# Sample attention of a two-layer decoder step: queries as stationary operand on four column quarters, one reversed scan, values of the own head

## The reference, cut to what matters

```python
z = jnp.einsum('bqkgd,bskd->bkgqs', qb, k) / math.sqrt(HEAD_DIM) + bias
mask = kpos[None, :] < qpos[:, None]
log_keep = jnp.where(mask, jax.nn.log_sigmoid(-z), 0.0)
suffix = lax.cumsum(log_keep, axis=4, reverse=True) - log_keep
attn = jnp.where(mask, jnp.exp(jax.nn.log_sigmoid(z) + suffix), 0.0)
o = jnp.einsum('bkgqs,bskd->bqkgd', attn, v)
```

## Time and profile before

| | us |
|---|---|
| median of 3 runs | 2024.17 (2018.96 to 2031.26) |
| the profiled execution | 2034.04 |
| its span | 2032.4 |
| in it: new tokens' part of the sample attention | 1581.6 to 1590.9 |
| pages' part of the sample attention | 1590.9 to 1787.6 |
| layer 1 out and the last norm | 1787.6 to 2032.4 |

### The profile page before, as it was taken

One profiled execution on the slowest core, in us unless ns is written; L12 is line 12 of the kernel. 1 busy time (PEld: TensorE's weight loads), 2 busy tenths in 40 slices (PEclk: granted clock), 3 DMA queues, 4 the chain that ended last, 5 costly groups with the idle time before them and its releaser, 6 DMA issues.

```text
span 2032.4 us, 35373 instructions
## 1 busy us (share of the span) xinstructions
PE 1847.5 (91%) x13466; PEld 1761.1 (87%) x13466; DVE 1126.7 (55%) x1844; ACT 785.6 (39%) x1132; POOL 272.0 (13%) x184
## 2 busy tenths in 40 slices
PE   4999999999997999947999999999997799899995
PEld 3899999999997999937989989999996676689993
DVE  4766666666666222296667577577576433442226
ACT  3244444444434222232555455465455222232222
POOL 4100000000000001133322322322321000001110
PEclk9999999999998999957999999999998677799995
DMA  5323232322322323342222222222224346412324
GB/s 194 95 88 89 84 92 83 90 85 84 92 67 59 92 83 92 106 151 83 76 61 63 85 63 69 79 73 63 84 63 133 106 146 181 148 53 85 91 84 154
DMA packets 278697, 191.50 MB, mean 94 GB/s; under 512 B 7899, under 2 KB 250715, under 8 KB 277979
## 3 DMA queue, kind: packets, MB, share of 16 engines
q1 hardware_dynamic: 277708, 188.03, 31.1%
q0 software_dynamic: 896, 2.23, 0.4%
HBM read 174.26 MB, written 15.97 MB: 94 GB/s over the span
## 4 chain that ended last, share of the span: by engine, by line
PE 74%; DVE 12%; issue 7%; ACT 6%; DMA 1%; POOL 0%; SPq 0%; ACTq 0%; DVEq 0%; POOLq 0%
PE PS L591 20%; PE PS L593 20%; PE PS L592 20%; PE Z L876 4%; PE PS L847 2%; PE PS L858 1%; PE Z L591 1%; PE Z L593 1%; PE Z L592 1%; DVE Y L1463 1%; ACT WS L937 1%; ACT L1122 1%; DVE WS L1241 1%; DMA prow<-in_state_h_dram 1%; DVE T L1503 1%
## 5 line engine op out<-in xcount | busy, mean ns | idle before, releaser
L591 PE MATMUL PS<-U,WS 128*128 128x272 f32 x3712 | 1089.3, 293 | 60.3 <-DVE U L1470 34.1
L593 PE MATMUL PS<-U,WS 128*128 128x272 f32 x3712 | 1085.2, 292 | 0.0
L592 PE MATMUL PS<-U,WS 128*128 128x272 f32 x3712 | 1081.7, 291 | 0.0
L591 PEld LDWEIGHTS PS<-U,WS 128*128 128x128 f32 x3712 | 712.0, 192 | 67.6 <-issue 35.5
L592 PEld LDWEIGHTS PS<-U,WS 128*128 128x128 f32 x3712 | 712.1, 192 | 0.8
L593 PEld LDWEIGHTS PS<-U,WS 128*128 128x128 f32 x3712 | 711.5, 192 | 0.0
L1241 DVE TENSOR_TENSOR WS<-raw,WS 128x1024 fp32r<-128x1024 f32 (+1 forms) x240 | 305.9, 1275 | 500.5 <-ACT WS L937 498.0
L937 ACT ACTIVATE WS<-raw 128x1024 fp32r<-128x1024 f32 (+1 forms) x240 | 246.7, 1028 | 601.8 <-PE PS L593 596.1
L506 POOL TENSOR_TENSOR raw<-raw,GN 128x1024 f32<-128x1024 f32 x80 | 159.6, 1996 | 436.2 <-DMA raw<-in_b_w_in_dram 340.6
L518 POOL TENSOR_TENSOR T<-T 128x544 f32<-128x544 f32 x60 | 88.4, 1473 | 379.4 <-ACT T L1033 376.9
L515 POOL COPY T<-T 128x544 f32<-128x544 f32 x4 | 3.2, 790 | 852.2 <-ACT T L1033 825.4
(11 more groups left out here) (212 smaller groups left out, 2025.9 us busy)
## 6 DMA issues: line engine op xcount, KB each, us to landing
raw<-in_a_w_in_dram SPq DMA_DIRECT2D x80, 512.0 KB, 3.8
raw<-in_b_w_in_dram SPq DMA_DIRECT2D x64, 512.0 KB, 4.1
raw<-in_a_w_out_dram SPq DMA_DIRECT2D x32, 512.0 KB, 3.8
raw<-in_b_w_out_dram SPq DMA_DIRECT2D x32, 512.0 KB, 3.8
KPG<-in_cache_k_dram SPq DMA_DIRECT2D x64, 256.0 KB, 2.9
VPG<-in_cache_v_dram SPq DMA_DIRECT2D x64, 256.0 KB, 2.9
T<-scratch_x SPq DMA_DIRECT2D x32, 272.0 KB, 2.9
scratch_x<-T SPq DMA_DIRECT2D x16, 272.0 KB, 2.1
```

Source lines behind the costliest of these rows:

```text
L591: pe.matmul(psum, w_hi, x_hi, start=first, stop=False)
L592: pe.matmul(psum, w_hi, x_lo, start=False, stop=False)
L593: return pe.matmul(psum, w_lo, x_hi, start=False, stop=last)
```

## The change

The sample attention is written anew; the projections, the prompt's attention and all else stay.

- One step is a half page position j (16 of them): four sequences. `key_turn` is the same four transposes per sequence. `scores` swaps the operands: the queries of one key/value head and sequence are stationary (32 columns, of which 16 are its own and 16 belong to the neighbour and are ignored), the 128 turned keys are the moving columns, and the four heads k write the partition quarters 32k to 32k+31 of one bank. Scores thus have queries on partitions and keys along the free axis.
- The later-key sum is one reversed `tensor_tensor_scan` over 512 elements (four sequences by 128 keys) on DVE, with a multiplier `RUN` that is 0 where a new sequence starts, and the carry of the page before added to the last key. The triangular products and the high and low split are gone.
- The weights must now be turned back (`weights_turn`, four transposes per half step) and copied by ACT (`weight_copy`) before `values`, which multiplies only the own head: 16 products per half step with 32 stationary columns and 128 moving ones, again on four partition quarters, accumulated over all pages in PSUM. `OA` and its additions are gone.
- Loads come in half steps of four pages, each with its own semaphore; keys of positions 1 and 2 first, then their values, then keys and values of the half steps in turn. The loop is unrolled and page numbers have fixed places.
- The new tokens are handled in 32-column tiles, with 32 small products and a handful of small DVE operations.

```diff
-                    for k in range(NKV):
-                        cols = slice(k * P + b * 16, k * P + b * 16 + 16)
-                        ins = pe.matmul(zs[:, slot, cols], KPT[:, b % 4, k * DH:(k + 1) * DH], QS[:, cols], start=True, stop=True)
+            def scores(c):
+                j, i = c // 4, c % 4
+                pe.wait_ge(kp_odd if c % 2 else kp_even, c // 2 + 1)
+                for k in range(NKV):
+                    ins = pe.matmul(SC[k * QW:(k + 1) * QW, j % 2, i * P:(i + 1) * P], query(k, j % 2 * 4 + i),
+                                    KPT[:, c % 4, k * DH:(k + 1) * DH], start=True, stop=True)
+                ins.then_inc(kp_used, 1)
-                for b in range(NB):
-                    v = VST[:, :] if isinstance(n, int) and n == 0 else VPG[:, slot, b, :]
-                    ins = pe.matmul(d_pair_bank(b // 2)[b % 2 * QR:(b % 2 + 1) * QR, :], T[:, 4, b * QR:(b + 1) * QR], v,
-                                    start=True, stop=True)
+            def weights_turn(j):
+                h = j % 2
+                pe.wait_ge(d_exp, j + 2)
+                pe.wait_ge(d_wt_out, j + 1)
+                for i in range(4):
+                    ins = pe.transpose(WT[:, h, i * P:(i + 1) * P], DW[h][:, i * P:(i + 1) * P], IDN[:])
+                ins.then_inc(d_wt, 1)
+            def weigh(h, i, b, v, first, last):
+                for k in range(NKV):
+                    ins = pe.matmul(OS[k * QW:(k + 1) * QW, h, i * P:(i + 1) * P], WPT[:, h, i * P + k * QW:i * P + (k + 1) * QW],
+                                    v[:, k * DH:(k + 1) * DH], start=first and i == 0, stop=last and i == 3, skip_group_check=True)
+                return ins
+            for j in range(NHALF):
+                half_scores(j)
...
+                if j >= 4:
+                    values(j - 4)
+                if j >= 3:
+                    weights_turn(j - 3)
+            def weight_copy(j):
+                act.wait_ge(d_wt, j + 2)
+                act.wait_ge(d_pv, j + 1)
+                nc.scalar.activation(WPT[:, j % 2, :], WT[:, j % 2], ACT.Copy).then_inc(d_wt_out, 1)
+            def run_sums(j):
+                V.tensor_tensor_scan(DI[j % 2][:, ::-1], RUN[:, ::-1], DL[j % 2][:, ::-1], 0.0, ALU.mult, ALU.add).then_inc(d_scan, 1)
+                dve.wait_ge(d_scan, j + 1)
+                V.tensor_tensor(DZ[j % 2], DZ[j % 2], DI[j % 2], ALU.subtract).then_inc(d_arg, 1)
+            def load_keys(n, h):
+                if n > 2:
+                    sp.wait_ge(kp_t, 8 * (n - 3) + 4 * h + 4)
+                load_pages(n, h, KPG, a["cache_k"], keys_in)
+            def load_values(n, h):
+                if n > 2:
+                    sp.wait_ge(d_pv, 2 * (n - 3) + h + 3)
+                load_pages(n, h, VPG, a["cache_v"], values_in)
```

More of the change, by code:

```diff
@@ L882, in _ @@
-            pe.wait_ge(strip_out, SE0)
-            for k in range(NKV):
-                ins = pe.matmul(zs[0:NS, 0, k * P:(k + 1) * P], KST[:, k, :], QS[:, k * P:(k + 1) * P], start=True, stop=True)
-            ins.then_inc(d_z, 1)
-            d_later_keys(0)
-            PAGES = 16 * NB
-            d_step(1, 1, PAGES, first=True)
-            with pe.Fori(1, NPAGE // 2) as i:
-                d_step(i * 2, 0, i * PAGES, i * PAGES)
-                d_step(i * 2 + 1, 1, i * PAGES + PAGES, i * PAGES)
@@ L902, in pair_e @@
+            for j in range(NHALF, NHALF + 4):
+                values(j - 4)
+                if j < NHALF + 3:
+                    weights_turn(j - 3)
+            for h in range(2):
+                pe.wait_ge(d_sums[h], 1)
+                for i in range(4):
+                    ins = pe.transpose(KT[:, h, i * P:(i + 1) * P], OE[h][:, i * P:(i + 1) * P], IDN[:])
+                ins.then_inc(d_turned, 1)
             def pair_e(i, first):
@@ L1196, in _, with key_copy @@
-            d_exps(0, NS)
-            with act.Fori(1, NPAGE + 1) as n:
-                steps.loop(n, 1, 2)
-                for b in range(0, NB, 2):
-                    act.wait_ge(kp_t, n * 8 + (b - 7))
-                    if b >= 4:
-                        act.wait_ge(kp_used, n * 8 + (b - 11))
-                    nc.scalar.activation(KPT[:, b % 4, :], d_bank(b), ACT.Copy).then_inc(kp_even, 1)
-                d_exps(n, P)
-            steps.leave(NPAGE)
+            def key_copy(c):
+                act.wait_ge(kp_t, c + 1)
+                if c >= 4:
+                    act.wait_ge(kp_used, c - 3)
+                nc.scalar.activation(KPT[:, c % 4, :], KT[:, c % 2], ACT.Copy).then_inc(kp_even, 1)
@@ L1208, in _ @@
+            act.wait_ge(d_pv, NHALF + 1)
+            nc.scalar.activation(OE[0], OS[:, 0], ACT.Copy).then_inc(d_sums[0], 1)
             act.wait_ge(d_out, 1)
@@ L1664, in _ @@
-            d_chain(0, 0, NS)
-            dve.wait_ge(d_cleared, 1)
-            with dve.Fori(0, NPAGE // 2) as i:
-                steps.loop(i, 0, 2)
-                for m in (1, 2):
-                    n = i * 2 + m
-                    for b in range(1, NB, 2):
-                        dve.wait_ge(kp_t, n * 8 + (b - 7))
-                        if b >= 4:
-                            dve.wait_ge(kp_used, n * 8 + (b - 11))
-                        V.tensor_copy(KPT[:, b % 4, :], d_bank(b)).then_inc(kp_odd, 1)
-                    d_chain(n, m % 2, P)
@@ new lines, in _ @@
+            new_tokens()
+            for j in range(NHALF + 2):
+                if j < NHALF:
+                    key_copy(4 * j + 1)
+                if j == 0:
+                    new_weights()
+                if 1 <= j <= NHALF:
+                    logits(j - 1)
+                if j >= 2:
+                    keep(j - 2)
+                if j < NHALF:
+                    key_copy(4 * j + 3)
+                if j >= 2:
+                    run_sums(j - 2)
+            dve.wait_ge(d_pv, NHALF + 2)
```

369 lines of the change are left out of this document (203 added, 166 removed).

## The result

The changed kernel takes 1959.32 us (median of 4 runs, 1956.68 to 1961.7), the kernel before took 2027.72 beside it: a ratio of 0.966 (95% interval 0.962 to 0.971), **68 us less**. The forecast was 42 us less, 1982; the time lies inside the range, and it is the time of the second rival (the clock stays at 2.4 GHz and SP's issuing binds, 1956).

What follows compares the result with a forecast made beforehand. PE was taken to bound the pages, with SP's issuing binding at the higher clock. Low-clock and high-clock sums gave gains of 16 and 68 us; the middle, 42 off 2024.17, gave 1982 us, range 1948 to 2014.

Steps and rivals of the forecast that it cites:

- the second rival: Pages' part: the clock stays at 2.4 GHz and SP's issuing of page loads binds; 68 us less, 1956 us; chance 0.2.
- PE bounds the pages, its work falls: Pages, per half step: PE's work falls from 8.2 to 5.1 us at 2.4 GHz, 9.4 us at 1.2 GHz.
- The quarters overlap fully: Scores and values on PE: four column quarters run side by side, 0.85 us each per half step, bounds 0.85 and 3.4.
- The price of the rival: Quarters not side by side: scores and values each 2.55 us more at 2.4 GHz, 5.1 at 1.2; about 2160 us; chance 0.07.
- Its threshold: Serial quarters turn the change into a loss once a half step costs over 12.3 us.
- Changes of shape: PE's switches between 128 and 32 columns, eight per half step: 0.15 us each at 2.4 GHz, 0.20 at 1.2.
- The hole: Between half steps PE waits for ACT's weight copy and key copy: 1.6 us each time.
- The start: New tokens' work ahead of the pages: 9.3 us as before, bounds 6 and 12, so pages begin at 1590.9.
- SP: SP's queue issues page loads at 1.105 us each, 8.8 us per half step, binding at the higher clock.
- The sum for the high clock: Pages' part at 2.4 GHz from step 1 on, paced by SP: the stage ends at 1720, a gain of 68 us.
- The clock: Pages' part: a mixed clock with a mean near 0.75, given 0.5, spread over 1962 to 2004 us.
- the middle of the two sums: Between stage ends of 1772 (all at 1.2 GHz) and 1720 (2.4 GHz): near 1746, 42 us less.

Runs made afterwards that it cites:

- one-quarter kernel: The changed kernel with a sequence's four score products on one column quarter and all value products of a half step on quarter 0: 2015.82 us, ratio 0.994.
- widened kernel before: The kernel before with 128 query columns instead of 16 streamed through each score product: 1995.46 us, ratio 0.987.

## Why the prediction was right, and where it was not

- **PE bounds the pages, its work falls.** Right. At 2.4 GHz the half step's work without the hole was forecast at 5.1 us and is 6.47 - 1.18 = 5.3 us. Key turns, scores, values and weight turns all lie within about 0.2 us of their terms; a sequence of turns and scores is 0.94 us where 0.44 + 0.21 + two changes of shape of 0.15 make 0.95.
- **The quarters overlap fully.** Right, 1.06 us for 32 records, where the two bounds were 0.85 and 3.4. The price of the rival was right too: 2.55 us more for each was forecast, and the one-quarter kernel shows 0.64 x 4 = 2.6 us for the scores. Its threshold was not: serial quarters leave the kernel just ahead of before, because the clock stays up (0.98), whereas I had them run at 1.2 GHz and lose 136 us. TensorE: Matmul & The Clock Gate in the Trainium skill (Part 3, The mechanism) says that weight loads go beside running products only where the row group differs. Here all products use all 128 rows, and a change of the column quarter alone takes a record with its load from 0.11 to 0.033 us, so the trace differs.
- **Changes of shape.** Idle PEld of 0.17 us ahead of scores and 0.20 ahead of turns, eight times in a half step; the term of 0.15 us each was right to within 0.05.
- **The hole.** The loop is as forecast, but 1.18 us rather than 1.6: ACT starts 0.04 us after PE's turn ends, and its second copy starts 0.49 us after the first (1650.53 to 1651.02) rather than 0.59 + 0.13. This is the term with the largest error on the path at 2.4 GHz, and the clock may have hung on it: with holes of 1.80 and of 2.44 us, and a longer second wait, the mean clock goes to 0.87 and 0.73.
- **The start.** 9.3 us was taken, with bounds of 6 and 12. The first turn stands 7.1 us earlier than before; the 64 small records of the new tokens (L904) take 1.03 us, and their DVE and ACT steps run beside the pages' first turns instead of ahead of them. From the end of the prompt's last product to the first turn it is 2.2 us (1582.58 to 1584.78), under the lower bound. That serial chain did not exist any more, which the bounds had missed.
- **SP.** Right: 1.12 us per page from 1620 to 1705 where 1.105 was taken, no pause, PE waiting for pages at the end. The sum for the high clock ended at 1720 from a start at 1590.9, 129 us; measured are 127.4.
- **The clock.** The step that failed: "I put the forecast at the middle of the two sums". It was 0.93, not 0.75. In the profiled executions, which the forecast went by, the stage ends 75 us earlier and not 42: 7 us of the 33 between are the start's, and nearly all of the other 26 the clock's. That the medians differ by just the 68 us of the second rival is in part luck: its sum lacked the 7 us of the start, and the profile that it was subtracted from was 6 us longer than the median beside the changed kernel. Two things told against the middle. The long stretch at 1.2 GHz in the earlier trace rows lay in the mixture of turns and 16-column products with full loads, which was to disappear; and the mean of before was carried over to a stream that shared little with it. The widened kernel before shows that this mixture cost 26 us (1 - 0.987, of 2020 us): a clock lost by the old form of the scores and not by the stage. The clock did fall twice on the way in the changed kernel. The first time was at 1607.2, with no wait for a page, behind a hole of 1.60 us between half steps 2 and 3, which have no values:

```profile
1605.57 0.66 PE L849 MATMUL PS<-IDN,KPG 128*128 128x128 f32 x4 [1.60 <-ACT KPT L1219]
...
1607.10 0.61 PE L863 MATMUL PS<-KPT,QS 128*32 128x128 f32 x8
1607.99 1.09 PE L849 MATMUL PS<-IDN,KPG 128*128 128x128 f32 x4 [0.28 <-ACT KPT L1219]
```

The second was behind SP's first long stall:

```profile
1677.30 1.11 PE L849 MATMUL PS<-IDN,KPG 128*128 128x128 f32 x4 [3.89 <-DMA KPG<-in_cache_k_dram]
1678.35 0.66 PE L863 MATMUL PS<-KPT,QS 128*32 128x128 f32 x8
...
1680.41 1.93 PE L887 MATMUL Z<-VPG,WPT 128*32 128x128 f32 x32
```

The stall was named as a reason for a fall, and it costs little here, because while SP sets the pace a slower PE only waits less. The rule of the Trainium skill that transposes do not count for the clock (TensorE: Matmul & The Clock Gate, Part 4, PE-mode transpose) finds no support in this trace: turns hold 0.59 of each 0.94 us of turns and scores (1645.19 to 1645.78), some 2.9 of the 5.3 us that PE works in a half step, and the clock stayed at 1.00 for 61 us. It is not refuted by that, since no kernel here ran with turns alone.

## What to carry to other kernels

Before a mean clock is carried over to a new form of a stage, look at which records stand in the stretches where it was low, and ask whether they will be there afterwards; here a stage at 0.76 became one at 0.93, and 128 columns in place of 16 did as much to the old kernel's clock by themselves. A chain in which two engines hand a result back and forth once per step is best kept short for two reasons: it costs its length, and TensorE's hole may cost clock on top. When a faster engine meets a queue that issues a transfer every 1.1 us, splitting the issuing between two queues gives back as much as making it cheaper.

## What the runs showed of the hardware

- Products of 32 stationary and 128 moving columns on the four column quarters cost 0.033 us per record at 2.4 GHz when neighbours use different quarters, 0.076 with four products in a row on one, and 0.11 with all on one.
- Widening a 16-column stream to 128 behind a load of 128 columns cost 0.05 us per eight records and raised the granted clock of the stage from 0.76 to 0.94.
- A stretch of 61 us with PE busy for 80% and a hole of 1.18 us in every 6.47 kept 2.4 GHz; holes of 2.44 us, with a second of up to 1.21, brought 1.2 GHz back in all but one of eleven half steps; the mean was 0.73, and 1.0 of the 10.0 us of a half step was the clock's.
- A change between 128 and 32 stationary columns left PEld idle for 0.17 to 0.20 us at 2.4 GHz.
- A page load with its lookup costs 1.10 us on SP and 1.15 us on GpSimd to issue; without the lookup four take 1.75 us on SP.
